# Hybrid encoder trunk in fp32: neighbouring tokens' scores made inside the attention, a block sweep with one level less

## The reference, cut to what matters

```
S_t = diag(exp(log_decay_t)) S_{t-1} + k_t v_t^T ;  o_t = S_t^T q_t        (per head, causal)

rel = b[i] - b[j]                               # b = running sum of the log decays
scores[i, j] = sum_d q[i, d] * k[j, d] * exp(rel[d])     # for j <= i
o_intra[i] = sum_j scores[i, j] * v[j]
```

## Time and profile before

| | before |
|---|---|
| median of 3 runs | 1460.27 us (1458.55 to 1460.65) |
| the profiled execution: its own time | 1460.37 us |
| its span, first to last instruction | 1458.6 us |
| mean granted clock of PE | 0.992 |
| busy: PE / PEld / DVE / ACT / POOL | 98% / 80% / 52% / 43% / 45% |

### The profile page before, as it was taken

One profiled execution on the slowest core, in us unless ns is written; L12 is line 12 of the kernel. 1 busy time (PEld: TensorE's weight loads), 2 busy tenths in 40 slices (PEclk: granted clock), 3 DMA queues, 4 the chain that ended last, 5 costly groups with the idle time before them and its releaser, 6 DMA issues.

```text
span 1458.6 us, 17094 instructions
## 1 busy us (share of the span) xinstructions
PE 1426.3 (98%) x6677; PEld 1164.7 (80%) x6677; DVE 761.1 (52%) x1132; ACT 629.2 (43%) x1091; POOL 652.6 (45%) x365
## 2 busy tenths in 40 slices
PE   8999999999999999999999999999999999999999
PEld 6878778886788888888878876887767888888887
DVE  5473584464766305663155536837547562156621
ACT  6746582655423212332346556635754322122221
POOL 4645353451444444344445354625424443444442
PEclk9999999999999999999999999999999999999999
DMA  6332002332233233323234210123312332333322
GB/s 172 100 89 68 20 21 81 116 102 58 72 105 98 94 94 102 101 87 107 75 87 116 73 58 15 59 72 114 90 58 87 87 102 94 94 102 96 105 81 94
DMA packets 174208, 125.64 MB, mean 86 GB/s; under 512 B 12562, under 2 KB 150577, under 8 KB 174129
## 3 DMA queue, kind: packets, MB, share of 16 engines
q1 hardware_dynamic: 173568, 124.55, 28.7%
q10 hardware_dynamic: 560, 0.01, 0.0%
HBM read 122.44 MB, written 2.10 MB: 85 GB/s over the span
## 4 chain that ended last, share of the span: by engine, by line
PE 89%; DVE 6%; ACT 3%; issue 1%; DMA 1%; POOL 0%; SPq 0%; ACTq 0%; DVEq 0%
PE bank L609 26%; PE bank L611 26%; PE bank L610 26%; PE bank L902 2%; PE bank L744 2%; PE bank L861 1%; PE bank L862 1%; PE bank L945 1%; PE bank L732 1%; DVE h L1554 1%; DVE x_lo L1488 1%; DVE scores_h L1743 1%; ACT cprobs L1118 1%; ACT h_sq L1095 1%; DMA raw<-in_w_in 1%
## 5 line engine op out<-in xcount | busy, mean ns | idle before, releaser
L536 POOL TENSOR_TENSOR w_lo<-raw,w_hi 128x1024 fp32r<-128x1024 f32 (+1 forms) x230 | 547.4, 2382 | 726.7 <-ACT w_hi L1073 726.6
L1073 ACT ACTIVATE w_hi<-raw 128x1024 fp32r<-128x1024 f32 (+1 forms) x230 | 237.5, 1035 | 343.6 <-PE bank L611 340.0
L609 PE MATMUL bank<-x_hi,w_hi 128*128 128x512 f32 (+1 forms) x944 | 372.8, 395 | 3.1 <-DVE x_lo L1544 1.4
L610 PE MATMUL bank<-x_lo,w_hi 128*128 128x512 f32 (+1 forms) x944 | 369.0, 391 | 0.0
L611 PE MATMUL bank<-x_hi,w_lo 128*128 128x512 f32 (+1 forms) x944 | 368.7, 391 | 0.0
L609 PEld LDWEIGHTS bank<-x_hi,w_hi 128*128 128x128 f32 (+1 forms) x944 | 177.7, 188 | 47.8 <-issue 5.0
L610 PEld LDWEIGHTS bank<-x_lo,w_hi 128*128 128x128 f32 (+1 forms) x944 | 177.6, 188 | 38.4 <-issue 1.4
L611 PEld LDWEIGHTS bank<-x_hi,w_lo 128*128 128x128 f32 (+1 forms) x944 | 177.5, 188 | 38.1
L1829 DVE SCALAR_TENSOR_TENSOR conv<-gate_in,gains_all,conv 128x512 f32<-128x512 f32 x44 | 120.5, 2739 | 1.5
L1420 ACT ACTIVATE conv_silu<-conv 128x512 f32<-128x512 f32 x44 | 27.8, 632 | 164.5 <-DVE conv L1830 164.5
L1825 DVE TENSOR_TENSOR gate_in<-bank,r_bc 128x512 f32<-128x512 f32 x44 | 30.4, 692 | 116.0 <-PE bank L611 110.0
(11 more groups left out here) (312 smaller groups left out, 2285.4 us busy)
## 6 DMA issues: line engine op xcount, KB each, us to landing
raw<-in_w_ffn_in SPq DMA_DIRECT2D x88, 512.0 KB, 3.8
raw<-in_w_ffn_out SPq DMA_DIRECT2D x40, 512.0 KB, 3.7
raw<-in_w_in SPq DMA_DIRECT2D x28, 512.0 KB, 3.8
raw<-in_w_mix_out SPq DMA_DIRECT2D x16, 512.0 KB, 3.8
raw<-in_w_ca_kv SPq DMA_DIRECT2D x32, 256.0 KB, 3.3
raw<-in_w_in SPq DMA_DIRECT2D x18, 256.0 KB, 3.0
raw<-in_w_ca_q SPq DMA_DIRECT2D x8, 512.0 KB, 3.7
raw<-in_w_ca_out SPq DMA_DIRECT2D x8, 512.0 KB, 3.8
```

The costliest lines, as they stand in the source:

```text
L536: pool.tensor_tensor(w_lo[gi % SPLIT][:, 0:n], raw[gi % RAW][:, 0:n], w_hi[gi % SPLIT][:, 0:n].bitcast(f32), ALU.subtract).then_inc(S["lo_ ...
L609: pe.matmul(o, ah, bh, start=first, stop=False)
L610: pe.matmul(o, ah, bl, start=False, stop=False)
L1073: act_.activation(w_hi[k % SPLIT][:, 0:n], raw[k % RAW][:, 0:n], ACT.Copy).then_inc(S["hi_split"], 1)
```

## The change

What it does:

1. Level m = 1 leaves the sweep (`LEVELS` begins at 2; `BLOCKS` keeps 1 for the decays and keys). The scores between a token of odd place and the one before it are instead made like the diagonal: POOL multiplies the odd queries with the even keys (`pair_products`) into the even places of `qk`, PE sums them with a second run of `diagonals`, in step 5 of the attention, ACT evacuates them, and `score_base` writes both values, through `pair_eye` (the identity with one more entry above each odd diagonal place), in the same four instructions per half.
2. `pair_products` also multiplies the even keys by the odd decays, which is the key step of level 1. DVE's first query products move from steps 5 and 6 to 3 and 4, since the pair product needs them; those of level 1 come in steps 7 and 8.
3. `scores_g` and `scores_h` now both lie over the rotary tables and small buffers (`rot_tab`, `r_diag`, `gate_tmp`, `kr_rot`, `kr_tok`), not over `x_lo`. So both `score_base` calls run in the attention, and `Qx` of x = 1 takes the place over `x_lo`. `qk` moves over `k_tok`, so it waits for the last key transposes.
4. The zeros of the second `Qx` pair are written by POOL at the start of `recurrences`, no longer by DVE. `EXPANDS` moves from step 8 to 9.
5. The first level of the sweep now waits for keys too, and is followed by a unit of the output projection; six such units stay in all.

```diff
-        LEVELS = (1, 2, 4, 8, 16, 32, 64)
+        pair_eye = sb("pair_eye", [P, P])
+        LEVELS = (2, 4, 8, 16, 32, 64)
+        BLOCKS = (1,) + LEVELS
...
-        scores_h = place("scores_h", 24, [P, NT, NH, P])
-        R0, R1, R2, R3, R4, R5 = 32, 48, 72, 80, 104, 125
+        R0, R1, R2, R3, R4, R5, R6 = 32, 48, 72, 80, 104, 125, 141
+        scores_g, scores_h = place("scores_g", R6, [P, NT, NH, P]), place("scores_h", R6 + 8, [P, NT, NH, P])
...
-        Qx = [[place(f"Qx{x}_{i}", kb, [P, NH, SEQ]) for i, kb in enumerate(((0, 8), (16, R0 + 8))[x])] for x in range(2)]
-        qk = place("qk", R0, [P, 3, SEQ])
+        Qx = [[place(f"Qx{x}_{i}", kb, [P, NH, SEQ]) for i, kb in enumerate((16 * x, 16 * x + 8))] for x in range(2)]
+        qk = place("qk", R3 + 12, [P, 3, SEQ])
...
-        EXPANDS = 8
+        EXPANDS = 9
...
+            def pair_products(pool, layer):
+
+                pool.wait_ge(S["q_level"], past(layer, "q_level") + 2)
+                pool.wait_ge(S["diag_mm"], past(layer, "diag_mm") + 1)
+                pairs_of_ = [a[:, :, :].rearrange("p f (b two) -> p f b two", two=2) for a in (qk, Q, K, decay)]
+                even, odd = [a[:, :, :, 0] for a in pairs_of_], [a[:, :, :, 1] for a in pairs_of_]
+                pool.tensor_tensor(even[0], odd[1], even[2], ALU.mult).then_inc(S["pair_prod"], 1)
+                pool.wait_ge(S["pair_prod"], past(layer, "pair_prod") + 1)
+                for f in (slice(0, 1), slice(1, 3)):
+                    pool.tensor_tensor(even[2][:, f], even[2][:, f], odd[3][:, f], ALU.mult).then_inc(S["k_level"], 1)
+
             def score_base(pool, x):
+                v = small[:, DIAG:DIAG + 16 * NT].rearrange("p (two n e) -> p n e two", two=2, n=NT)
                 for n in range(NT):
-                    c = DIAG + 8 * n + NH * x
-                    pool.tensor_tensor((scores_g, scores_h)[x][:, n], ident[:, :].unsqueeze(1).to_broadcast([P, NH, P]),
-                                       small[:, c:c + NH].unsqueeze(2).to_broadcast([P, NH, P]), ALU.mult
+                    pool.tensor_tensor((scores_g, scores_h)[x][:, n].rearrange("p h (c two) -> p h c two", two=2),
+                                       pair_eye[:, :].rearrange("p (c two) -> p c two", two=2).unsqueeze(1).to_broadcast([P, NH, P // 2, 2]),
+                                       v[:, n, NH * x:NH * (x + 1), :].unsqueeze(2).to_broadcast([P, NH, P // 2, 2]), ALU.mult
                                        ).then_inc(S["scores_base"], 1)
 
-            def first_query_zeros(pool, layer):
-                pool.wait_ge(S["diag_evac"], past(layer, "diag_evac") + 1)
+            def score_bases(pool, layer):
+                pool.wait_ge(S["diag_evac"], past(layer, "diag_evac") + 2)
                 score_base(pool, 0)
                 pool.wait_ge(S["cig_half"], past(layer, "cig_half") + 1)
                 for x in range(2):
                     pool.memset(Qx[x][0][:, :, :], 0.0).then_inc(S["zeroed"], 1)
+                score_base(pool, 1)
 
             def recurrences(pool, layer):
 
+                pool.wait_ge(S["score_mm"], past(layer, "score_mm") + MLA_ITEMS)
+                pool.memset(state[:, :, :], 0.0).then_inc(S["zeroed"], 1)
                 pool.wait_ge(S["tok_mm"], past(layer, "tok_mm") + 2 * NT)
-                score_base(pool, 1)
+                for x in range(2):
+                    pool.memset(Qx[x][1][:, :, :], 0.0).then_inc(S["zeroed"], 1)
...
                         if i == slab_at["cig", 0]:
-                            pool.wait_ge(S["v_mm"], past(layer, "v_mm") + NT)
+                            pool.wait_ge(S["qkT_mm"], past(layer, "qkT_mm") + 4 * NT)
...
                         if i == slab_at["cig", 3]:
-                            first_query_zeros(pool, layer)
+                            pair_products(pool, layer)
+                            score_bases(pool, layer)
...
                     def dense_between(i):
-                        if i == 2:
-                            diagonals()
+                        if i in (2, 5):
+                            diagonals(i == 5)
...
-                            if li:
-                                pe.wait_ge(S["k_level"], past(layer, "k_level") + 2 * (li - 1) + x + 1)
+                            pe.wait_ge(S["k_level"], past(layer, "k_level") + 2 * li + x + 1)
...
-                        if li:
-                            mix_units("sweep")
+                        mix_units("sweep")
...
                     def attention_between(i):
+                        if i in (2, 5):
+                            pair = i == 5
+                            act_.wait_ge(S["diag_mm"], past(layer, "diag_mm") + pair + 1)
+                            c = DIAG + 8 * NT * pair
+                            act_.activation(small[:, c:c + 8 * NT], pb[3][:, 0:8 * NT], ACT.Copy).then_inc(S["diag_evac"], 1)
...
                     def first_queries(i):
-                        if i == 5:
+                        if i == 3:
                             dve.wait_ge(S["qk_prod"], past(layer, "qk_prod") + 1)
                             dve.wait_ge(S["gate_done"], past(layer, "gate_done") + 1)
-                        if i in (5, 6):
-                            next_queries(i - 5, 0)
-                        if i == MLA_ITEMS + 2:
-                            dve.wait_ge(S["tok_mm"], past(layer, "tok_mm") + 2 * NT)
-                            dve.memset(Qx[0][1][:, :, :], 0.0).then_inc(S["zeroed_v"], 1)
-                        if i == MLA_ITEMS + 3:
-                            dve.wait_ge(S["probsT_mm"], past(layer, "probsT_mm") + MLA_ITEMS)
-                            dve.memset(Qx[1][1][:, :, :], 0.0).then_inc(S["zeroed_v"], 1)
+                        if i in (3, 4):
+                            next_queries(i - 3, 0)
+                        if i == 7:
+                            dve.wait_ge(S["pair_prod"], past(layer, "pair_prod") + 1)
+                        if i in (7, 8):
+                            next_queries(i - 7, 1)
```

More of the change, by code:

```diff
@@ L465, in block_decays @@
                 pool.wait_ge(S["gate_done"], past(layer, "gate_done") + 1)
-                for li, m in enumerate(LEVELS):
+                for li, m in enumerate(BLOCKS):
                     d = block_decay(m, slice(0, P), slice(0, 3)).rearrange("p f (b two) -> p f b two", two=2)
@@ L512, in _ @@
                                    base=0, pattern=[[-1, P]], channel_multiplier=1).then_inc(S["identity_done"], 1)
+                pool.wait_ge(S["identity_done"], 1)
+                eyes = [a[:, :].rearrange("p (c two) -> p c two", two=2) for a in (pair_eye, ident)]
+                pool.tensor_copy(eyes[0][:, :, 0], eyes[1][:, :, 0])
+                pool.tensor_tensor(eyes[0][:, :, 1], eyes[1][:, :, 0], eyes[1][:, :, 1], ALU.add)
                 link(pool.memset(head_of[:, :], 0.0))
@@ L835, in _, with diagonals @@
                             transpose_qk(1, (2 * k - 10, 2 * k - 9))
-                    def diagonals():
+                    def diagonals(pair):
                         claim(3)
-                        pe.wait_ge(S["qk_prod"], past(layer, "qk_prod") + 1)
+                        if pair:
+                            pe.wait_ge(S["pair_prod"], past(layer, "pair_prod") + 1)
+                        else:
+                            pe.wait_ge(S["qk_prod"], past(layer, "qk_prod") + 1)
                         for n in range(NT):
@@ L845, in diagonals @@
                         mark(mm, S["diag_mm"])
-                        freed[3] = (S["diag_evac"], past(layer, "diag_evac") + 1)
+                        freed[3] = (S["diag_evac"], past(layer, "diag_evac") + pair + 1)
                     def dense_between(i):
-                        if i == 2:
-                            diagonals()
+                        if i in (2, 5):
+                            diagonals(i == 5)
                         first = sum(CIG_UNITS.get(j, 0) for j in range(i))
@@ L932, in _ @@
                         pe.wait_ge(S["swept"], past(layer, "swept") + 4 * len(LEVELS))
-                        pe.wait_ge(S["q_level"], past(layer, "q_level") + 2 * len(LEVELS) + 2)
+                        pe.wait_ge(S["q_level"], past(layer, "q_level") + 2 * len(LEVELS) + 4)
                         if n == 1:
@@ L1285, in attention_between @@
                     def attention_between(i):
+                        if i in (2, 5):
[3 more added lines that the diff above has]
+                            act_.activation(small[:, c:c + 8 * NT], pb[3][:, 0:8 * NT], ACT.Copy).then_inc(S["diag_evac"], 1)
                         if i == 2:
-                            act_.wait_ge(S["diag_mm"], past(layer, "diag_mm") + 1)
-                            act_.activation(small[:, DIAG:DIAG + 8 * NT], pb[3][:, 0:8 * NT], ACT.Copy).then_inc(S["diag_evac"], 1)
                             ahead(("cig", 1))
@@ L1295, in attention_between @@
```

(2 more changed lines are left out.)

38 lines of the change are left out of this document (16 added, 22 removed).

## The result

The changed kernel takes 1470.45 us (median of 4 runs, 1469.45 to 1472.17), the kernel before 1460.46 beside it (4 runs, 1458.55 to 1462.92): a ratio of 1.0069, interval 1.0056 to 1.0081. The forecast was 1456.4 with a range of 1453.0 to 1460.6; the time is 10 us above that range, and 14 above the forecast. The profiled execution took 1469.45 us with a span of 1467.7, 9.1 longer than the span before (1458.6).

A forecast was written before the change was run, and what follows sets the result against it. PE was taken as the bound, busy 98% of the span with 89% of the chain. Sweep -14.8, diagonals +5.2, wait +2.4 and clock +3.2 made -4.0 us, from 1460.37 to 1456.4 us, range 1453.0 to 1460.6.

The forecast's parts named there:

- edits costed at nothing: POOL and DVE work under PE's dense units, delayed `qk`, setup and new tensor placement: no added time on PE.
- The sweep: Level 1 and PE's idle time for POOL's keys go: 7.4 us gained per layer, 14.8 in all; bounds 5.0 to 8.2.
- The second diagonals: Attention step 5: 24 more PE entries cost 2.60 us per layer, 5.2 in all; bounds 2.5 to 3.0.
- The wait ahead of them: Attention step 5: PE waits for POOL's pair product, 1.4 us in layer 0, 1.0 in layer 1; 2.4 in all.
- The clock after the pairs: Attention, after step 5's pair diagonals: one clock fall per layer, 1.6 us each, 3.2 in all; between 0 and 3.4.
- GpSimd's bases: POOL's score bases in the attention: about 4.2 us each, or an estimated 6 by the skill; no effect on the sum.
- the 15 us of cover: POOL finishes projection slab 0 about 170, PE wants it in the sweep at 187; this slack absorbs POOL's added work.
- The slower rival: Attention steps 7 to 9: POOL blocks DVE, PE loses 4 us or more per layer; 1464.4 us or above, chance 0.10.
- the rival with a smaller gain: Sweep: PE finds DVE's copies and ACT's expansions late, levels gain 5.0 to 6.0; 1459 to 1461 us, chance 0.25.
- the local sum: Changed places in sweep and attention together, both layers: -14.8 + 5.2 + 2.4 + 3.2 = -4.0 us.

The follow-up runs named there:

- the last variant: Changed kernel with 448 bytes of padding before the arena, first diagonals split over steps 2 and 3, pair diagonals moved to steps 7 and 8: 1450.01 us.
- the padded kernel: Changed kernel with an unused 448-byte tensor in front of the arena, nothing else: 1459.47 us, ratio 0.9998 to the kernel before.

## Why the prediction was wrong

- **The step that failed** is the last of the edits costed at nothing: "The new placement adds no wait: the tables are dead until the next layer." It looked at when tiles are alive, and not at where they lie. Moving the rotary tables into the arena and taking out tensors ahead of it shifted the arena against the weight tiles from a multiple of 256 bytes to 64 beyond one. The 5005 distances measured then took 3.5 ns more on the mean, 17.5 us in all. Undone by 448 bytes, it is 11.0 us of the median (1470.45 to 1459.47), less than 17.5 since the clock then falls more often (a mean of 0.987 to 0.995 over its ten executions, 0.993 to 0.995 over the four of the changed kernel). No view of the profile before could show this price.
- **The sweep:** 8.2 and 7.7 us gained in place of 7.4; level 4 waits 0.92 us for ACT's expansion, as laid out (1.0). Inside the bounds, layer 0 at the upper one.
- **The second diagonals:** 2.91 and 2.81 us, for 2.60, inside 2.5 to 3.0.
- **The wait ahead of them:** 1.65 and 1.27 for 1.4 and 1.0. The chain was right (DVE's second query product, then POOL), the term too small: the pair product took 2.15 us, not the 1.47 of the row chosen as nearest. That one reads interleaved elements and writes adjacent ones; the pair product writes interleaved ones too, which is the difference I see and did not test.
- **The clock after the pairs:** a fall in each layer, as said (153.2 to 156.7 and 876.8 to 880.3), and none in the first level. What the sum lacked is that falls elsewhere are no constant: in all 7 before, 4 after, 11 with the padding and 2 in the last variant, at 1.7 us each.
- **GpSimd's bases:** 5.46 and 5.89 us, against an estimated 6 by the Trainium skill, GPSIMD Engine Reference, section 7, and 4.2 by the old row. The trace agrees with the page's direction; the 15 us of cover took it, as forecast.
- **The slower rival** had the sign and not the mechanism: PE waits nowhere in steps 7 to 9. The number of the rival with a smaller gain, 1459 to 1461, is where the kernel stands at the old placement, and for another reason: the falls.

Taken for itself, then, the local sum held to 0.3 us (-3.7 for -4.0), in part by luck: the sweep gave 1.1 more than forecast and the attention cost 1.4 more. The time was missed by a term that was put at nothing.

## What to carry to other kernels

When a change adds, drops or resizes any tensor ahead of others, print the addresses of the operands of the hottest matmuls before and after, and hold the distance between streamed and stationary tiles at a multiple of 256 bytes, the only fast one of the three remainders tried here, with a pad if need be; measure the change at equal placement before judging it. When work far from the change gets slower, count instructions in an equal stretch of both traces first: it shows in one view what no wait and no chain shows. Count the falls of the granted clock in both traces as well, and try narrow matmuls away from a wait, between dense units. Run such variants several times: the executions of one kernel here lay up to 9 us apart, the slow ones at a lower mean clock.

## What the runs showed of the hardware

- A 512-column fp32r product took 0.2271 us from start to start with the arena a multiple of 256 bytes from the weight tiles, 0.2307 at 64 beyond it and 0.2330 at 128. The 0.2307 is a mixture of long stretches at 0.2289 and others at 0.2333; what decides between them is open. In time 64 beyond costs the kernel before 0.9% (1.0088, 1.0068 to 1.0107).
- One odd distance slows more than the products in which that tile streams or is loaded: with only w_lo off, x_lo by w_hi and x_hi by w_lo were slow, x_hi by w_hi was not.
- With the changed kernel's order the clock fell less often at the slower pace: 4 falls in the changed kernel as it stood, 11, 7 and 8 in three with the fast placement (448, 960 and 192 bytes), one profile of each. In the kernel before no such difference shows: its mean clock was 0.991 to 0.995, and 0.993 to 0.995 with 64 bytes. How much of this is the pace is not settled.
- After 1.3 us of waiting and 24 narrow entries the clock of one execution stayed at its lower level for 6.9 us on end, while PE was busy all the time (155.3 to 162.2 of the padded kernel); after 12 narrow entries with no wait ahead of them it stayed at 1.00 (157.0 to 160.5 and 161.9 to 165.4 of the last variant).
